# Seven block products in place of eight for two row pairs of the first gate and value chunks

## The chip, the cores and the metric

The program runs on one core of a Trainium2 chip. The metric is the device time of one execution in microseconds (us); lower is better.

## The reference, cut to what matters

A layer of a streaming encoder is computed for 256 tokens of width 2048. Its first step projects the normalised tokens by one wide weight matrix, and the first 4096 columns of that are the two halves of a gated unit:

```
h = rms_norm(x, norm_mix_g)                 # 256 x 2048
z = h @ w_in                                # 2048 x 9280 weights
u_conv, c_q, c_kv, k_pe, gate_logits = split(z)
a, gate = split(u_conv, 2)                  # 2048 columns each
h = a * sigmoid(gate)                       # then a depthwise convolution, and so on
```

Convolution, latent attention, a cross attention and a squared-ReLU MLP (width 8192) follow; the change leaves them alone.

## The kernel before

All engines are programmed by hand; every instruction's place on its queue is written out, and semaphores tie the queues together. The width 2048 is 16 tiles of 128 rows (`k`), the tokens are two halves of 128 (`t`), and the projection is made in chunks of 512 columns. Of chunk `i` the gate columns (`COL_G`) and the value columns (`COL_A`) are made one after the other, so 8 chunks of products make `u_conv`. A chunk's weights come in 8 **units** of two row tiles (128 x 1024, 512 KB). Unit `n` passes through these hands:

- SP loads it into slot `n % 4` of `raw` (`load`, L478). It first waits until VectorE is done with the unit four before.
- ScalarE (ACT) rounds it to the matmul's format, `whi` (`hi`, L717). It waits for the landing and until TensorE is done with the unit four before (`used`).
- VectorE (DVE) makes the rest, `wlo = raw - whi` (`lo`, L1213).
- TensorE (PE) multiplies (`unit`, L1979 to L1981): for each row tile and token half three matmuls, x high by w high, x high by w low, x low by w high, of 128 x 128 tokens by 128 x 512 weights; 12 matmuls a unit. Each token half has its own PSUM bank: 2 and 3 for the gate, 0 and 1 for the value.

The tokens arrive as rows (`x_in`, four chunks of 512 columns), and are transposed by TensorE (`turn`, L1992, 8 transposes a chunk into banks 6 and 7), scaled and rounded by ACT (`turn_out`, L734, `a_hi`) and split by DVE (`turn_low`, L1234, `a_lo`). `X_BEFORE` says before which units the chunks are turned, `X_AFTER` after which unit's `hi` and `lo` ACT and DVE take them out.

So the program's first stage is units 0 to 7 (gate, all 16 row tiles), a few small transposes into banks 5 and 4 (L2065, L2068), units 8 to 15 (value), and from unit 16 a loop over the other chunks that begins with a wait for `sg_ready`. Between the units ACT squares the tokens for the norm (`square_sums`, L749), takes the root (L758, with a table load) and, after unit 7, the sigmoid (L763); DVE multiplies at the end (`glu`, L1251). POOL loads small vectors and then computes the rotary angles (L631 to L654), which ACT needs at L825.

Later in the program, in the MLP, row pairs are already multiplied in Strassen's way, with seven products for eight. DVE makes the sums of four weight blocks in place (`t_sums`, L1830 to L1834), ACT rounds them (`t_high`, L1115), DVE splits them (`t_low`, L1839); sums of the tokens are made likewise, and the results are mixed out of PSUM (`m_sums`, L1846 to L1854). Their rows serve as prices here. "Rows" of the weights below means row tiles.

Of the kernel before, what the change touches and what calls it, by code (L numbers as in the profile page):

```python
# [8 lines left out]
ALU = mybir.AluOpType  # L9
# [8 lines left out]
P = 128  # L18
D = 2048
# [105 lines left out]
X_BEFORE, X_AFTER = (1, 3, 5), (2, 4, 6)  # L125
# [33 lines left out]
SLOTS = 3  # L159
B11, B12, B21, B22 = T1, T3, T4, T2 = range(4)  # L160
# [67 lines left out]
def build(nc, x, mem, positions, norm_mix_g, w_in, b_gate, conv_w, conv_b, conv_ln_g, conv_ln_b,  # L228
# [9 lines left out]
    with ExitStack() as ctx:  # L238
# [32 lines left out]
        sq_x = at(o + nbytes([P, D]), "sq_x", [P, TT, D])  # L271
# [63 lines left out]
        cy_copy = at(c_base + 28672, "cy_copy", [P, TT, NC])  # L335
        early = Sevens(cw_sum, ((cs_c[0], cs_m[0]), (cs_c[2], cs_m[2])), ((cs_c[1], cs_m[1]), (cs_c[3], cs_m[3])),
# [12 lines left out]
        rows = take("rows", [P, 2, TT, NC])  # L349
        qz = at(o, "qz", [P, 2, SEQ])  # L350
# [66 lines left out]
        ckv_whole = sem("ckv_whole")  # L417
        kpe_out, kpe_ready, kpe_prod, kpe_rotated, kpe_turned, kpeT_ready = (sem(n) for n in ("kpe_out", "kpe_ready", "kpe_prod", "kpe_rotated", "kpe_turned", "kpeT_ready"))
# [55 lines left out]
        def _(sp):  # L474
# [23 lines left out]
            for k in range(1, UPC):  # L498
                load(U_CONV + k, 0, w_in[:, 2 * k:2 * k + 2, COL_G:COL_G + NC])
                if k in (1, 2, 4):  # L500
                    load_x((1, 2, 4).index(k) + 1)
            load_chunk(U_CONV + UPC, 0, w_in, COL_A)
# [46 lines left out]
            def load_blocks(g, j):  # L549
# [3 lines left out]
                if j < SLOTS:  # L553
                    sp.wait_ge(chunk_out, g * CH + N_FF)
                else:
                    sp.wait_ge(m_done, g * FJ + (j - SLOTS + 1))
# [36 lines left out]
        def _(pool):  # L593
# [35 lines left out]
            pool.dma_start(cw_rows[CONV_K:CONV_K + 1, :], conv_b).then_inc(cw_landed, 16)  # L629
            pool.wait_ge(pos_landed, 16)  # L630
# [72 lines left out]
            pool.wait_ge(m_done, FJ_ALL)  # L703
# [7 lines left out]
        def _(act):  # L711
# [77 lines left out]
            for k in range(1, UPC):  # L789
                hi(U_CONV + k)  # L790
                if k in X_AFTER:
                    c = X_AFTER.index(k) + 1
                    turn_out(T_X + c, a_hi, CPB * c, V_MIX)
# [318 lines left out]
            def t_high(g, j):  # L1112

                act.wait_ge(t_made, g * (3 * FJ) + 3 * (j + 1))
                act.activation(t_hi[j % SLOTS][:], t_raw[j % SLOTS][:], ACT.Copy).then_inc(t_hi_ready, 1)  # L1115

# [91 lines left out]
        def _(dve):  # L1208
# [113 lines left out]
            for k in range(1, UPC):  # L1322
                lo(U_CONV + k)
                if k in X_AFTER:
                    c = X_AFTER.index(k) + 1
                    turn_low(T_X + c, a_lo, a_hi, CPB * c, V_MIX)
            lo(8)
            for k in range(6, 2 * UPC):
                lo(U_CONV + k + LEAD)
                if k == 8:  # L1330
                    reciprocal(rs_x, sd_x, R_X)
                if k == 10:
                    dve.wait_ge(vec_turned, 2)
                    dve.tensor_copy(vec[:, KT:], ps[:, 5, KT:V_N]).then_inc(vec_ready, 1)
                    dve.wait_ge(cw_turned, 1)
                    dve.tensor_copy(cw[:].rearrange("p k s -> p (k s)"), ps[:, 4, :]).then_inc(conv_step, 1)
            dve.wait_ge(used, U_CONV + 2 * UPC)
            dve.wait_ge(sg_ready, 1)
            dve.wait_ge(rs_ready, R_X)
            glu()  # L1340
# [485 lines left out]
            def t_sums(g, j):  # L1826

                t, done = t_raw[j % SLOTS], 3 * j
# [821 lines left out]
```

## Time and profile before

| what | value |
|---|---|
| median of three runs | 1595.53 us (1595.01 to 1596.44) |
| the profiled execution's own time | 1594.99 us |
| its span, first to last instruction | 1592.7 us |
| busy PE / DVE / ACT / POOL | 1581.0 / 1309.1 / 902.9 / 94.2 us |
| granted TensorE clock, mean | 0.998 |

The span is what the trace covers; 2.3 us of the execution's own time lie around it. A busy PE does not mean that it is at its peak, since a matmul's row runs on after the next one has begun.

### The profile page before, as it was taken

What the parts mean: (1) busy time and instruction counts of PE and PEld (TensorE: products, weight loads), DVE (VectorE), ACT (ScalarE), POOL (GpSimd) and SP (SyncE); (2) the same over time, 40 slices, a digit from 0 to 9 for tenths busy, and PEclk for the clock granted to TensorE, in tenths of its full rate; (3) what the DMA queues carried; (4) which work ended last, traced back from release to release, by engine and by line L of the source; (5) the groups of instructions that cost most, each with busy time, mean ns of one, the idle gap of its engine ahead of it and who ended that gap; (6) DMA issues with size and microseconds to landing.
All of it is one profiled execution on the core that took longest, in us unless ns stands there. A gap on an engine that the chain in (4) does not pass through costs nothing.

```text
span 1592.7 us, 22193 instructions
## 1 busy us (share of the span) xinstructions
PE 1581.0 (99%) x7909; PEld 1341.3 (84%) x7909; DVE 1309.1 (82%) x1757; ACT 902.9 (57%) x1138; POOL 94.2 (6%) x174
## 2 busy tenths in 40 slices
PE   9999999999999999999999999999999999999997
PEld 7888888888888888888888888888888888888886
DVE  5588999999998998787997786886779776978687
ACT  7444456555555556754566666455655565546655
POOL 6500010000000000000000000000000000000001
PEclk9999999999999999999999999999999999999999
DMA  7666655655655666657664676888678867887694
GB/s 259 200 189 186 192 160 177 175 181 172 185 174 174 209 201 185 197 177 243 216 197 146 184 228 185 281 261 289 180 259 266 271 212 221 281 272 225 205 295 147
DMA packets 169581, 336.68 MB, mean 211 GB/s; under 512 B 10377, under 2 KB 23297, under 8 KB 169089
## 3 DMA queue, kind: packets, MB, share of 16 engines
q1 hardware_dynamic: 164608, 324.84, 65.0%
q0 software_dynamic: 4864, 10.80, 3.1%
q8 instruction: 50, 0.82, 0.2%
q14 instruction: 27, 0.22, 0.0%
q10 hardware_dynamic: 32, 0.01, 0.0%
HBM read 326.16 MB, written 2.10 MB: 206 GB/s over the span
## 4 chain that ended last, share of the span: by engine, by line
PE 98%; DVE 0%; ACT 0%; issue 0%; ACTq 0%; POOL 0%; POOLq 0%; DVEq 0%
PE ps L2566 15%; PE ps L1979 12%; PE ps L1981 12%; PE ps L1980 12%; PE ps L2257 9%; PE ps L2259 9%; PE ps L2258 9%; PE ps L2568 7%; PE ps L1992 1%; PE ps L2168 1%; PE ps L2393 1%; PE ps L2163 1%; PE ps L2146 1%; PE ps L2148 1%; PE ps L2147 1%; PE ps L2202 1%
## 5 line engine op out<-in xcount | busy, mean ns | idle before, releaser
L717 ACT ACTIVATE w_both<-raw 128x1024 fp32r<-128x1024 f32 x522 | 550.6, 1059 | 488.1 <-PE ps L1981 176.4
L1213 DVE TENSOR_TENSOR w_both<-raw,w_both 128x1024 fp32r<-128x1024 f32 x522 | 634.8, 1223 | 192.5 <-ACT w_both L717 190.4
L2566 PE MATMUL ps<-a_both,w_both 128*128 128x512 f32 x1024 | 321.6, 395 | 0.0
L1979 PE MATMUL ps<-w_both,a_both 128*128 128x512 f32 (+1 forms) x636 | 251.3, 395 | 0.1
L1981 PE MATMUL ps<-w_both,a_both 128*128 128x512 f32 (+1 forms) x636 | 247.0, 388 | 0.0
L1980 PE MATMUL ps<-w_both,a_both 128*128 128x512 f32 (+1 forms) x636 | 247.0, 388 | 0.0
L2568 PEld LDWEIGHTS ps<-a_both,w_both 128*128 128x128 f32 x1024 | 192.4, 188 | 45.4
L1274 DVE SCALAR_TENSOR_TENSOR acc<-hconv,cwk,acc 128x256 f32<-128x256 f32 x464 | 201.3, 488 | 7.7 <-PE ps L2202 7.6
L2568 PE MATMUL ps<-a_both,w_both 128*128 128x256 f32 x1024 | 201.1, 278 | 0.0
L2257 PE MATMUL ps<-w_both,c_hi 128*128 128x512 f32 x402 | 156.8, 390 | 0.0
L2259 PE MATMUL ps<-w_both,c_lo 128*128 128x512 f32 x402 | 156.4, 389 | 0.0
L2566 PEld LDWEIGHTS ps<-a_both,w_both 128*128 128x128 f32 x1024 | 156.2, 189 | 0.3
L2258 PE MATMUL ps<-w_both,c_hi 128*128 128x512 f32 x402 | 156.4, 389 | 0.0
L1981 PEld LDWEIGHTS ps<-w_both,a_both 128*128 128x128 f32 x636 | 119.4, 188 | 24.5
L1979 PEld LDWEIGHTS ps<-w_both,a_both 128*128 128x128 f32 x636 | 119.5, 188 | 23.1 <-issue 0.3
L1980 PEld LDWEIGHTS ps<-w_both,a_both 128*128 128x128 f32 x636 | 119.6, 188 | 22.5
L2257 PEld LDWEIGHTS ps<-w_both,c_hi 128*128 128x128 f32 x402 | 75.5, 188 | 16.2 <-DVE w_both L1213 0.8
L2259 PEld LDWEIGHTS ps<-w_both,c_lo 128*128 128x128 f32 x402 | 75.5, 188 | 15.8
L2258 PEld LDWEIGHTS ps<-w_both,c_hi 128*128 128x128 f32 x402 | 75.5, 188 | 15.4
L1839 DVE TENSOR_TENSOR t_lo<-t_raw,t_hi 128x2048 fp32r<-128x2048 f32 x31 | 71.0, 2291 | 13.7 <-ACT t_hi L1115 13.6
L1115 ACT ACTIVATE t_hi<-t_raw 128x2048 fp32r<-128x2048 f32 x31 | 59.1, 1906 | 1.7 <-DVE t_raw L1834 1.5
L697 POOL DMA_DIRECT2D xres<-m_sum x7 | 8.4, 1197 | 819.2 <-DVE xres L1675 819.2
(441 smaller groups left out, 2243.3 us busy)
## 6 DMA issues: line engine op xcount, KB each, us to landing
raw<-in_w_ff_dram SPq DMA_DIRECT2D x225, 512.0 KB, 4.6
raw<-in_w_in_dram SPq DMA_DIRECT2D x137, 512.0 KB, 3.9
t_raw<-in_w_ff_dram SPq DMA_DIRECT2D x31, 1024.0 KB, 7.2
raw<-in_w_mla_out_dram SPq DMA_DIRECT2D x32, 512.0 KB, 4.3
raw<-in_w_conv_out_dram SPq DMA_DIRECT2D x32, 512.0 KB, 4.4
raw<-in_w_out_dram SPq DMA_DIRECT2D x32, 512.0 KB, 4.5
raw<-in_w_ukv_dram SPq DMA_DIRECT2D x16, 512.0 KB, 3.8
raw<-in_w_xkv_dram SPq DMA_DIRECT2D x16, 512.0 KB, 4.0
```

The costliest lines, as they stand in the source:

```text
L717: act.activation(whi[:, s, :], raw[:, s, :], ACT.Copy).then_inc(hi_ready, 1)
L1213: dve.tensor_tensor(wlo[:, s, :], raw[:, s, :], whi[:, s, :].bitcast(F32), ALU.subtract).then_inc(lo_ready, 1)
L1274: ins = dve.scalar_tensor_tensor(out=to, in0=h[:, tap:tap + SEQ], scalar=cwk[:, tap:tap + 1], in1=to, op0=ALU.mult, op1=ALU.add)
L1839: dve.tensor_tensor(t_lo[j % SLOTS][:], t_raw[j % SLOTS][:], t_hi[j % SLOTS][:].bitcast(F32), ALU.subtract).then_inc(t_lo_ready, 1)
L1979: pe.matmul(sum_, x_hi[:, k0 + k, tok], w_hi, start=(first and k == 0), stop=False)
L1980: pe.matmul(sum_, x_hi[:, k0 + k, tok], w_lo, start=False, stop=False)
L1981: mm = pe.matmul(sum_, x_lo[:, k0 + k, tok], w_hi, start=False, stop=(last and k == kts - 1))
L2257: pe.matmul(ps[:, bank, :], x_hi, w_hi, start=first, stop=False, skip_group_check=True)
L2258: pe.matmul(ps[:, bank, :], x_hi, w_lo, start=False, stop=False, skip_group_check=True)
L2259: return pe.matmul(ps[:, bank, :], x_lo, w_hi, start=False, stop=last, skip_group_check=True)
L2566: pe.matmul(both, whi[:, s, cols[n]], a_both[:, :, k0 + k, :], start=(first and k == 0), stop=False)
L2568: mm = pe.matmul(ps[:, b0 + b + n, 0:SEQ], wlo[:, s, cols[n]], a_hi[:, k0 + k, :], start=False, stop=(last and k == 1))
```

## The change

Gate and value chunks of the first 512 columns are computed together. Rows 0 to 11 go as before (gate units 0 to 5, value units 6, 7, 8, 11, 14, 15). For the two row pairs 12/13 and 14/15 the four blocks (gate and value columns of an even and an odd row) are multiplied by both token halves in seven block products (21 matmuls) where eight (24) stood. A pair takes two slots, `left` (units 9 and 12, the two gate blocks, 6 matmuls) and `right` (units 10 and 13, the odd value block, 3 matmuls from the slot and 12 from the weight sums).

For this, SP loads the pair's four blocks once more, raw, into `e_raw` (two loads of 512 KB behind unit 5 and two behind unit 8); DVE makes three sums of them (`e_sums`), ACT rounds (`e_high`, 128 x 2048), DVE splits (`e_low`). ACT takes the last token chunk out of PSUM twice, rounded and whole (`turn_out_whole`), behind unit 7 instead of 6; DVE makes the tokens' sums (`eh_sums`), ACT rounds, DVE splits. The squares and the root move from behind units 7 and 8 to behind unit 14. The gate is no longer ready after unit 7: it is mixed from five banks by `em_sums` behind unit 16's `lo`, the sigmoid runs on the mixed rows, the small transposes wait for the mixing (they use its banks), and POOL's angles wait for the last product of the pairs.

```
-X_BEFORE, X_AFTER = (1, 3, 5), (2, 4, 6)
+X_BEFORE, X_AFTER = (1, 3, 5), (2, 4, 7)
+EM = 2
+E_PLAIN = KT - 2 * EM
+E_UNITS = ([("gate", m) for m in range(E_PLAIN // 2)]
+           + [("value", 0), ("value", 1), ("value", 2), ("left", 0), ("right", 0), ("value", 3), ("left", 1), ("right", 1), ("value", 4), ("value", 5)])
+E_LOAD = {5: 0, 8: 1}
+E_M1, E_M7, E_M6, E_M5 = 4, 5, 6, 7
...
+                if n in E_LOAD:
+                    j = E_LOAD[n]
...
+                    kts = slice(E_PLAIN + 2 * j, E_PLAIN + 2 * j + 2)
+                    sp.dma_start(e_raw[j % SLOTS][:, B11:B21 + 1:2, :], w_in[:, kts, COL_G:COL_G + NC]).then_inc(t_landed[j % SLOTS], 16)
+                    sp.dma_start(e_raw[j % SLOTS][:, B12:B22 + 1:2, :], w_in[:, kts, COL_A:COL_A + NC]).then_inc(t_landed[j % SLOTS], 16)
...
+            pool.wait_ge(m_done, EM)
             pool.wait_ge(pos_landed, 16)
...
-            square_sums(sq_x, x_in, ss_x)
-            hi(8)
-            act.wait_ge(ss_ready, SS_X)
-            root(sd_x, ss_x, D)
-            for k in range(6, 2 * UPC):
-                hi(U_CONV + k + LEAD)
-                if k == 9:
-                    act.wait_ge(used, U_CONV + UPC)
-                    act.wait_ge(rs_ready, R_X)
-                    glu_gate()
...
+            for n in range(1, 2 * UPC + LEAD):
+                if n < 2 * UPC and E_UNITS[n][0] == "right":
+                    hi_second(U_CONV + n, 0)
+                else:
+                    hi(U_CONV + n)
...
+                if n == 8:
+                    e_high(0)
+                if n == 9:
+                    eh_high(0)
+                if n == 12:
+                    e_high(1)
+                if n == 14:
+                    for t in range(TT):
+                        wait(act, ss_ready, t)
+                        act.activation(sq_x[:], x_in[:, t, :], ACT.Square, accum_out=ss_x[:, t:t + 1]).then_inc(ss_ready, 1)
+                    act.wait_ge(ss_ready, SS_X)
+                    root(sd_x, ss_x, D)
+                if n == 16:
+                    act.wait_ge(used, U_CONV + 2 * UPC - 3)
+                    act.activation(rows[:, 1, 0, :], ps[:, E_M1, :], ACT.Copy).then_inc(em_copied, 1)
+            act.wait_ge(sg_ready, 1)
...
+            def em_sums():
+
+                both, minus = rows[:, 1, :, :], rows[:, 0, :, :]
+                dve.wait_ge(em_copied, 1)
+                dve.wait_ge(m_done, EM)
+                dve.tensor_tensor(both[:, 1, :], ps[:, E_M6, :], both[:, 0, :], ALU.add).then_inc(em_made, 1)
...
+                dve.tensor_tensor(both, ps[:, 2:4, :], both, ALU.add).then_inc(sg_ready, 1)
+
+            for n in range(1, 2 * UPC + LEAD):
+                if n == 2 * UPC + 1:
+                    em_sums()
...
+                if n == 7:
+                    e_sums(0)
+                if n in X_AFTER:
+                    c = X_AFTER.index(n) + 1
                     turn_low(T_X + c, a_lo, a_hi, CPB * c, V_MIX)
...
+                if n == 8:
+                    eh_sums(0)
+                if n == 9:
+                    eh_low(0)
+                    e_low(0)
+                if n == 11:
+                    e_sums(1)
+                if n == 16:
                     reciprocal(rs_x, sd_x, R_X)
...
+                if n == 13:
+                    e_low(1)
...
+                elif kind == "right":
+                    pe.wait_ge(eh_lo_ready, m // 2 + 1)
+                    product(0, *e_combined(3, m), *e_slot(n, 1)).then_inc(used, 1)
...
+                    pe.wait_ge(t_lo_ready, m + 1)
+                    product(E_M6, *e_combined(1, m), *e_weight(T2, m), first=(m == 0), last=(m == EM - 1))
...
+            pe.wait_ge(em_made, 4)
             pe.wait_ge(vec_landed, 16 * 7)
```

**DVE between the last token chunk and the sums of the second pair.** Before, the low halves of the chunk (L1234), five units' `lo` in a row, and the reciprocal of the norm:

```order
L1234 SCALAR_TENSOR_TENSOR a_both<-ps,vec,a_both 128x256 [waits turn_hi]
L1234 SCALAR_TENSOR_TENSOR a_both<-ps,vec,a_both 128x256
L1213 TENSOR_TENSOR w_both<-raw,w_both 128x1024 [waits hi_ready] x5
L1241 RECIPROCAL stat<-stat 128x2 [waits sd_ready]
L1213 TENSOR_TENSOR w_both<-raw,w_both 128x1024 [waits hi_ready] x2
```

Now, from unit 8's `lo` on (L1282); the weight sums of the first pair and the chunk's low halves stand just ahead of these rows, behind unit 7's `lo`:

```order
L1282 TENSOR_TENSOR w_both<-raw,w_both 128x1024 [waits hi_ready]
L1397 TENSOR_TENSOR eh_sum_153<-e_act 128x256 [waits turn_hi]
L1398 TENSOR_TENSOR eh_sum_153<-e_act 128x256
L1400 SCALAR_TENSOR_TENSOR eh_sum_153<-eh_sum_153,e_act 128x256 [waits eh_made]
L1402 TENSOR_TENSOR eh_sum_153<-e_act,eh_sum_153 128x256 [waits eh_made]
L1282 TENSOR_TENSOR w_both<-raw,w_both 128x1024 [waits hi_ready]
L1407 TENSOR_TENSOR eh_lo_155<-eh_sum_153,eh_hi_151 128x1024 [waits eh_hi_ready]
L1422 TENSOR_TENSOR e_lo_145<-e_raw_142,e_hi_148 128x2048 [waits t_hi_ready]
L1288 TENSOR_TENSOR w_both<-raw,w_both 128x512 [waits hi_ready]
L1282 TENSOR_TENSOR w_both<-raw,w_both 128x1024 [waits hi_ready]
L1413 TENSOR_TENSOR e_raw_143<-e_raw_143 128x1024 [waits t_landed1]
```

Six instructions now stand between unit 8's `lo` and the half `lo` of unit 10 (L1288) that the first pair's `right` products wait for, besides unit 9's own.

**ACT around the squares.** Before, behind unit 7's `hi`:

```order
L717 ACTIVATE w_both<-raw 128x1024 [waits used,landed3]
L749 ACTIVATE sq_x,stat<-x_in 128x2048 x2
L717 ACTIVATE w_both<-raw 128x1024 [waits used,landed0]
L758 ACT_TABLE_LOAD
L758 ACTIVATE stat<-stat 128x2 [waits ss_ready]
L717 ACTIVATE w_both<-raw 128x1024 [waits used,landed1]
```

Now, from the rounding of the second pair's weight sums (L840) to the copy of the first mixed bank (L867); the L750 in the middle are units 14, 15 and 16:

```order
L840 ACTIVATE e_hi_149<-e_raw_143 128x2048 [waits t_made]
L757 ACTIVATE w_both<-raw 128x512 [waits used,landed1]
L750 ACTIVATE w_both<-raw 128x1024 [waits used,landed2]
L862 ACTIVATE sq_x,stat<-x_in 128x2048
L862 ACTIVATE sq_x,stat<-x_in 128x2048 [waits ss_ready]
L791 ACT_TABLE_LOAD
L791 ACTIVATE stat<-stat 128x2 [waits ss_ready]
L750 ACTIVATE w_both<-raw 128x1024 [waits used,landed3]
L750 ACTIVATE w_both<-raw 128x1024 [waits used,landed0]
L867 ACTIVATE rows<-ps 128x512 [waits used]
```

Both squares, the table load and the root stand between units 14 and 15, with no unit in between.

**PE at the small transposes.** Before, between the gate's last unit and the value's first:

```order
L1981 MATMUL ps<-w_both,a_both 128x512
L2065 MATMUL ps<-ident,vec_rows 128x104 [waits vec_ready,vec_landed]
L2068 MATMUL ps<-ident,cw_rows 128x32 [waits cw_landed]
L2068 MATMUL ps<-ident,cw_rows 128x32 x15
L1979 MATMUL ps<-w_both,a_both 128x512 [waits lo_ready]
```

Now, between unit 15 and the loop over the other chunks:

```order
L2193 MATMUL ps<-w_both,a_both 128x512
L2247 MATMUL ps<-ident,vec_rows 128x104 [waits vec_ready,vec_landed,em_made]
L2250 MATMUL ps<-ident,cw_rows 128x32 [waits cw_landed]
L2250 MATMUL ps<-ident,cw_rows 128x32 x15
L2254 UNCONDITIONAL_BRANCH
L2108 ISA [waits sg_ready]
L2114 MATMUL ps<-w_both,a_both 128x512 [waits lo_ready]
```

The transposes have gained a wait for `em_made`, the fourth of DVE's mixing sums; all later work of PE is queued behind it.

## Rows read from the trace of the kernel before

**Rows 1.** The page: span, and each engine's busy time.

```profile
span 1592.7 us, 22193 instructions
PE 1581.0 (99%) x7909; PEld 1341.3 (84%) x7909; DVE 1309.1 (82%) x1757; ACT 902.9 (57%) x1138; POOL 94.2 (6%) x174
```

**Rows 2.** Waits of PE's weight loads from 11 us on: total us, times, longest.

```profile
PEld ps L2257 <- DVE w_both L1213: 0.8, 2, 0.4
...
```

**Rows 3.** Timeline of PE: start us, us, engine, line, operation, shapes.

```profile
32.39 0.25 PE L2065 MATMUL ps<-ident,vec_rows 104*128 104x104 f32 x1
...
33.68 0.50 PE L1979 MATMUL ps<-w_both,a_both 128*128 128x512 f32 x1
...
36.53 0.39 PE L1979 MATMUL ps<-w_both,a_both 128*128 128x512 f32 x1
...
54.90 0.39 PE L1979 MATMUL ps<-w_both,a_both 128*128 128x512 f32 x1
```

**Rows 4.** Stretch of the start: PE, PEld, DVE, ACT, POOL busy, PEclk, DMA share, GB/s.

```profile
11.00:19.00 8.00, 7.87 (x40) 6.30 (x38) 5.81 (x10) 5.98 (x11) 1.98 (x4) 1.00 1.06 388
```

**Rows 5.** Issue of units 7 and 8 on SP's timeline, KB and us to landing.

```profile
16.00 0.37 SPq L478 DMA_DIRECT2D raw<-in_w_in_dram  x1
raw<-in_w_in_dram SPq DMA_DIRECT2D x1, 512.0 KB, 4.4
17.36 0.37 SPq L478 DMA_DIRECT2D raw<-in_w_in_dram  x1
raw<-in_w_in_dram SPq DMA_DIRECT2D x1, 512.0 KB, 5.8
```

**Rows 6.** DMA queues from 17 to 24 us: packets, MB, share of 16 engines.

```profile
...
q8 instruction: 1, 0.02, 1.0%
```

**Rows 7.** Timeline of ACT: copying out a chunk, a square, the root, two `hi`.

```profile
23.97 1.57 ACT L734 ACTIVATE a_both<-ps,vec 128x256 fp32r<-128x256 f32 x4 [2.90 <-PE ps L1992]
...
26.36 1.93 ACT L749 ACTIVATE sq_x<-x_in 128x2048 f32<-128x2048 f32 x1
...
31.23 1.28 ACT L758 ACT_TABLE_LOAD   x1
32.52 0.30 ACT L758 ACTIVATE stat<-stat 128x2 f32<-128x2 f32 x1
32.73 2.00 ACT L717 ACTIVATE w_both<-raw 128x1024 fp32r<-128x1024 f32 x2
```

**Rows 8.** Timeline of DVE in the first stage: two `lo`, a chunk, a wait.

```profile
20.16 2.36 DVE L1213 TENSOR_TENSOR w_both<-raw,w_both 128x1024 fp32r<-128x1024 f32 x2
24.84 1.66 DVE L1234 SCALAR_TENSOR_TENSOR a_both<-ps,vec,a_both 128x256 fp32r<-128x256 f32 x4 [2.32 <-ACT a_both L734]
...
31.25 1.23 DVE L1213 TENSOR_TENSOR w_both<-raw,w_both 128x1024 fp32r<-128x1024 f32 x1 [3.50 <-ACT w_both L717]
```

**Rows 9.** DVE in the MLP: three weight sums, then `lo`; four mixing sums, then the next.

```profile
916.87 1.22 DVE L1830 TENSOR_TENSOR t_raw<-t_raw 128x1024 f32<-128x1024 f32 x1
...
919.46 2.36 DVE L1213 TENSOR_TENSOR w_both<-raw,w_both 128x1024 fp32r<-128x1024 f32 x2
...
1024.47 0.68 DVE L1846 TENSOR_TENSOR m_sum<-ps,m_sum 128x512 f32<-128x512 f32 x1
...
1027.11 1.22 DVE L1675 TENSOR_TENSOR xres<-ps,xres 128x1024 f32<-128x1024 f32 x1
```

**Rows 10.** By tile: rounding and splitting of weight sums, token sums (ns min/median/max).

```profile
L1115 ACT ACTIVATE t_hi<-t_raw x31: 1897/1902/1925, 920.0 to 1555.7; 128x2048 fp32r<-128x2048 f32 x31
L1839 DVE TENSOR_TENSOR t_lo<-t_raw,t_hi x31: 2284/2292/2296, 921.9 to 1557.8; 128x2048 fp32r<-128x2048 f32 x31
L1531 DVE TENSOR_TENSOR h_sum<-h_sum,ps x2: 420/421/422, 716.2 to 717.0; 128x256 f32<-128x256 f32 x2
```

**Rows 11.** POOL's angles by tile, and ACT's use of them on its timeline.

```profile
L645 POOL TENSOR_SCALAR rope_tmp<-rope_tmp x12: 372/374/1371, 26.6 to 61.2; 128x64 f32<-128x64 f32 x12
203.25 0.31 ACT L825 ACTIVATE rope_cs<-rope_cs 128x128 f32<-128x128 f32 x1
```

More of the change, by code:

```diff
@@ L159 @@
 SLOTS = 3
+E_BLOCKS = [len(range(n, EM, SLOTS)) for n in range(SLOTS)]
 B11, B12, B21, B22 = T1, T3, T4, T2 = range(4)
@@ L804, in _ @@
+            act.wait_ge(sg_ready, 1)
+            act.wait_ge(rs_ready, R_X)
+            for t in range(TT):
+                last = act.activation(rows[:, 1, t, :], rows[:, 1, t, :], ACT.Sigmoid, scale=rs_x[:, t:t + 1])
+            last.then_inc(em_copied, 1)
             act.wait_ge(consts, 4)
@@ L1337, in _ @@
             dve.wait_ge(used, U_CONV + 2 * UPC)
-            dve.wait_ge(sg_ready, 1)
+            dve.wait_ge(em_made, 4)
+            dve.tensor_tensor(rows[:, 0, :, :], ps[:, 0:2, :], rows[:, 0, :, :], ALU.add).then_inc(em_made, 1)
+            dve.wait_ge(em_made, 5)
+            dve.wait_ge(em_copied, 2)
             dve.wait_ge(rs_ready, R_X)
-            glu()
+            for t in range(TT):
+                last = dve.scalar_tensor_tensor(out=rows[:, 0, t, :], in0=rows[:, 0, t, :], scalar=rs_x[:, t:t + 1],
+                                                in1=rows[:, 1, t, :], op0=ALU.mult, op1=ALU.mult)
@@ L2054, in _, with product @@
             first_product(1, 1, a_lo, whi).then_inc(used, 1)
-            for k in range(1, UPC):
-                if k in X_BEFORE:
-                    c = X_BEFORE.index(k) + 1
+            def product(bank, x_hi, x_lo, w_hi, w_lo, first=False, last=False):
+                pe.matmul(ps[:, bank, :], x_hi, w_hi, start=first, stop=False, skip_group_check=True)
+                pe.matmul(ps[:, bank, :], x_hi, w_lo, start=False, stop=False, skip_group_check=True)
+                return pe.matmul(ps[:, bank, :], x_lo, w_hi, start=False, stop=last, skip_group_check=True)
@@ L2058, in _ @@
+            for n in range(1, 2 * UPC):
+                if n in X_BEFORE:
+                    c = X_BEFORE.index(n) + 1
                     pe.wait_ge(x_landed[c], 16)
                     turn(T_X + c, x_in, NC * c, split_out(T_X + c - 1))
-                pe.wait_ge(turn_lo, k + 1)
-                unit(U_CONV + k, 0, a_hi, a_lo, 2 * k, 2, k == 0, k == UPC - 1)
+                kind, m = E_UNITS[n]
+                left, right = E_PLAIN + 2 * m, E_PLAIN + 2 * m + 1
+                if kind == "gate":
+                    pe.wait_ge(turn_lo, n + 1)
+                pe.wait_ge(lo_ready, U_CONV + n + 1)
+                if kind == "gate":
+                    for k in range(2):
+                        for t in range(TT):
+                            mm = product(2 + t, *tokens(2 * m + k, t), *e_slot(n, k))
+                    mm.then_inc(used, 1)
+                elif kind == "left":
+                    pe.wait_ge(turn_lo, left // 2 + 1)
+                    product(E_M1, *tokens(left, 0), *e_slot(n, 0), first=(m == 0), last=(m == EM - 1))
+                    product(2, *tokens(right, 0), *e_slot(n, 1), last=(m == EM - 1)).then_inc(used, 1)
+                elif kind == "right":
+                    pe.wait_ge(eh_lo_ready, m // 2 + 1)
+                    product(0, *e_combined(3, m), *e_slot(n, 1)).then_inc(used, 1)
+                    if m == 0:
+                        pe.wait_ge(turn_lo, 2 * CH)
+                    pe.wait_ge(t_lo_ready, m + 1)
+                    product(E_M6, *e_combined(1, m), *e_weight(T2, m), first=(m == 0), last=(m == EM - 1))
+                    product(3, *tokens(right, 1), *e_weight(T4, m), last=(m == EM - 1))
+                    product(E_M5, *e_combined(0, m), *e_weight(T1, m), first=(m == 0), last=(m == EM - 1))
+                    product(E_M7, *e_combined(2, m), *e_weight(T3, m), first=(m == 0), last=(m == EM - 1)).then_inc(m_done, 1)
+                else:
+                    for k in range(2):
+                        for t in range(TT):
+                            mm = product(t, *tokens(2 * m + k, t), *e_slot(n, k), first=(m == 0 and k == 0), last=(n == 2 * UPC - 1 and k == 1))
+                    mm.then_inc(used, 1)
@@ L2070, in _ @@
             tr.then_inc(cw_turned, 1)
-            for k in range(UPC):
-                unit(U_CONV + UPC + k, 0, a_hi, a_lo, 2 * k, 0, k == 0, k == UPC - 1)
             with pe.Fori(1, CH) as i:
```

142 lines of the change are left out of this document (105 added, 37 removed).

## The prediction

> **What bounds the kernel now.** I read the page first: PE is busy for 1581.0 us of a span of 1592.7, DVE for 1309.1 [rows 1]. Busy is not the same as full, so the second look is at PE's waits. From 11 us on the longest kind adds up to 0.8 us in two places [rows 2], so PE is fed all the way and every matmul that goes is worth its step in the stream. The step is read from starts, not from durations: from 36.53 to 54.90 us stand 81 steps [rows 3], 0.2268 us each, while one row lasts 0.39. The third look is at who feeds PE in the first stage. DMA runs at 388 GB/s, full, up to 19 us [rows 4]; ACT and DVE had room, with DVE idle 3.50 us before one `lo` [rows 8]. The change spends that room. So the question is whether DVE and ACT, in the new order, still keep ahead of PE.
>
> **The gain.** Seven products for eight, for two pairs: 2 x 3 = 6 matmuls less, 6 x 0.2268 = 1.36 us. Nothing else leaves PE: the chunk turns stay at units 1, 3 and 5 and the small transposes (32.39 to 33.68, 1.29 us [rows 3]) only move. 1.36 us is the most that can be won, and 0.2% of the time, about what a measurement of this kernel can tell from no change, is 3.2 us.
>
> **When PE would get there.** Before, unit 9 starts at 36.53, behind nine units and the transposes, so unit 16 starts at 36.53 + 84 x 0.2268 = 55.58. Now, with no wait, the first `right` would start at 36.53 - 1.29 + 6 x 0.2268 = 36.60, the transposes at 55.58 - 1.29 - 1.36 = 52.93, unit 16 at 54.22.
>
> **What SP adds.** Unit 7 was issued at 16.00 and landed 4.4 us later, at 20.4 [rows 5]. The first `e_raw` block, two loads of 512 KB, now goes ahead of units 6 and 7 into a queue that is full: 2 x 524 KB / 388 GB/s = 2.7 us [rows 4], so unit 7 lands at 23.1. That is the lower bound. The upper one comes from unit 8, which took 5.8 instead of 4.4 us [rows 5] though it moves no more: in that stretch an instruction load [rows 6] and POOL's small vectors come in between, and a unit has landed only when all sixteen parts have. If the same 1.4 to 1.5 us hit the longer queue, unit 7 lands at 24.6. I take 24.0, nearer to the row with the disturbance, since the queue now has work behind it throughout that stretch and the lost time can't be made up in an idle moment as before.
>
> The Trainium skill ("DMA: Bandwidth & Descriptors", Issuing engines are not separate DMA queues) says that transfers run on the same 16 engines and interleave, whichever engine started them. It speaks against the change: POOL's loads would take their turns out of the new block's time. The late unit 8 agrees. By the queue's bytes alone the sum below is +2.0 us; with the disturbance it is +2.9.
>
> **What DVE and ACT add: one chain from that landing to the transposes.** Steps are start to start. `hi` of unit 7 takes 1.06, so its `lo` starts 1.1 after the landing. DVE then never waits: `lo` 7 1.14 (2.36 for two, of which the last lasts 1.22 [rows 8]); the weight sums 2.59 (916.87 to 919.46 [rows 9]); the chunk's low halves 1.6 [rows 8]; `lo` 8 1.14; the tokens' sums four times 0.42 [rows 10], overlapped 1.5; `lo` 9 1.14; `eh_low`, of `lo`'s shape, 1.14; `e_low` 2.2 (2.29 [rows 10] less the overlap); half of a `lo` for unit 10, 0.6. Sum 13.1, and the half `lo` ends 14.2 after the landing. Had unit 7 landed at 23.1 that is 37.3: the first `right` waits 0.8; with 24.0 it waits 1.7.
>
> On: `lo` 11 1.14 and the second weight sums 2.59 end 18.0 after the landing. Now ACT is the one that is waited for: it rounds the sums (1.90 [rows 10], step 1.8), unit 13's half 0.55, unit 14's `hi` 0.95 (2.00 for two [rows 7]), two squares of 1.93 and a handoff 3.95, table load and root 1.28 + 0.30 [rows 7], stepping in 1.5, `hi` of unit 15 1.06: 9.8, at 27.8. Then DVE: `lo` 15 and 16 2.3, the reciprocal 0.15, four mixing sums (1024.47 to 1027.11 [rows 9]) with the last one's end 2.75: at 33.0, with handoffs 33.1. The copy of the first bank on ACT hides beside `lo` 16, the double copy of the last chunk (four pieces 1.57 [rows 7], so eight 3.1) beside the weight sums; without that cover it would cost the 1.6.
>
> Nothing in this chain waits for PE, so its length stands: the transposes can start at 24.0 + 33.1 = 57.1, unit 16 at 58.4 to 58.5, against 55.58: **+2.9 us**. With 23.1 it is +2.0, with 24.6 +3.5. Seen from PE these are four waits: about 1.7 at the first `right`, 1.0 at the second pair's sums (its `e_low` ends some 2.3 behind the sums' rounding), 0.3 at unit 15, whose `lo` stands behind the squares, and 1.2 at the transposes; 4.2 less 1.36. Each earlier wait only shortens the later ones; the last one sets the end.
>
> After that PE is not late again: `lo` 17 ends 2.3 behind the fourth mixing sum (the fifth, of 1.22, and its own 1.14), and is wanted 1.3 + 2.7 behind it; sigmoid, product and copies stand ahead of `lo` 19, wanted some 10 us behind it. So the shift stays as it is to the end. POOL's new wait moves the angles by some 27 us, from 23 to 50; ACT wants them at 203.25, and twelve of their operations lie from 26.6 to 61.2 [rows 11], so they end by some 95 and 100 us are spare.
>
> The bounds of the rest: some thirty steps, each read to about 0.03 us, make 0.9 us either way if all err to one side. With the landing's bounds the chain gives +1.1 to +4.4. The profiled execution took 1594.99 us, 2.3 around its span; with 2.9 it would be 1597.9, and the median lies 0.54 above that execution: **1598.4 us**.
>
> **Rivals.**
>
> *DVE and ACT keep up, and the saving shows.* Then no wait is left and the time is 1595.5 - 1.4 = 1594.2. It decides at one point: the fourth mixing sum must end by 52.9, so the chain would have to be 29.8 us long instead of 33.1 even with the earliest landing. For it speaks that the kernel's own rows of the same steps in the MLP run hidden; against it that there they stand among units with slack, and that the sum has no idle time left to squeeze. 1 in 9.
>
> *The landing is later, or the steps longer than read.* Unit 7 at 24.4 or later, or the added work on DVE slowed, makes it +3.2 or more, over 0.2%: 1599.3 or so (+3.8). For it speaks unit 8's row; against it that the disturbance lasted some 3 us there and may fall behind unit 7. 3 in 10.
>
> *POOL against DVE.* POOL's angles used to run beside a DVE with room; now they run from 50 us on, into the convolution's sums. One POOL operation goes from 372 ns to 1371 [rows 11] while a DVE subtraction is under way, so the two hold each other up; if DVE lost 0.1 us on each of four instructions of a unit, `lo` would fall behind 0.4 us a unit less its idle time, and over some fifteen units PE could wait 1 to 2 us more, 1600. The Trainium skill ("GPSIMD Engine Reference", Specifications) says that POOL shares its SBUF interface with VectorE and contends with instructions that have two SBUF inputs, as these have. It is POOL that the row shows late, not DVE. 1 in 50.
>
> **Chances and range.** The forecast, +1.1 to +3.2: 0.57; later and over +3.2: 0.30; the saving shows: 0.11; POOL: 0.02. The forecast and the saving both lie within 0.2%, which makes 0.67 same and 0.31 slower; nothing worked out here reaches -3.2, and I leave 0.02 for it. For eight in ten the range goes from just under the forecast's low end, where part of the saving would show, to +4.6: 1595.6 to 1600.1.
>
> **What would show it.** Right: in the changed profile PE has gaps of a microsecond or two ahead of the first `right`'s product and ahead of the transposes, the latter ended by a mixing sum; DVE has no idle time from unit 7's `lo` to the second weight sums; unit 7 lands near 24; unit 16 starts near 58.5; from there the two traces run parallel. Wrong: PE fed through, with unit 16 at 54.2; a wait of DVE for a landing in the middle of the chain; gaps on PE after 60 us. The prediction fails if the chain's steps overlap better than read one by one, or if DVE's work on the new tiles costs other than on the MLP's.

## The result, and the profile after

| | before | after |
|---|---|---|
| median of 13 runs each | 1595.44 us (1595.01 to 1596.44) | 1599.52 us (1598.82 to 1601.51) |
| the profiled execution's own time | 1594.99 us | 1599.33 us |
| its span | 1592.7 us | 1597.5 us |
| granted TensorE clock, mean | 0.998 | 0.997 |

The ratio is 1.0026, with a 95% interval of 1.0017 to 1.0034: 4.1 us slower, where 2.9 was forecast.

The same view as [rows 2], PE's weight loads of the changed kernel and what they waited for from 11 us on (total us, times, longest):

```profile
PEld ps L2191 <- DVE w_both L1288: 2.7, 1, 2.7
PEld ps L2191 <- DVE w_both L1282: 1.6, 4, 0.6
PEld ps L2247 <- DVE rows L1435: 1.0, 1, 1.0
```

Two waits are new, and both are where the prediction put one: L1288 is the half `lo` of the first `right`, L1435 the fourth mixing sum, for which the transposes wait. The waits expected at the second pair's sums and at unit 15 are missing; a small one ahead of unit 8, 0.3 us of PE's time, was not forecast. PE's timeline, which answers to [rows 3], shows the two, and one thing that nobody expected:

```profile
36.47 0.39 PE L2193 MATMUL ps<-w_both,a_both 128*128 128x512 f32 x1
39.10 0.79 PE L2191 MATMUL ps<-w_both,eh_hi 128*128 128x512 f32 x1 [2.25 <-DVE w_both L1288]
39.70 0.63 PE L2192 MATMUL ps<-w_both,eh_hi 128*128 128x512 f32 x1
40.12 0.63 PE L2193 MATMUL ps<-w_both,eh_lo 128*128 128x512 f32 x1
...
42.26 0.49 PE L2192 MATMUL ps<-e_lo,a_both 128*128 128x512 f32 x1
42.59 0.40 PE L2193 MATMUL ps<-e_hi,a_both 128*128 128x512 f32 x1
42.82 0.40 PE L2191 MATMUL ps<-e_hi,eh_hi 128*128 128x512 f32 x1
...
56.91 0.39 PE L2193 MATMUL ps<-w_both,a_both 128*128 128x512 f32 x1
57.85 0.31 PE L2247 MATMUL ps<-ident,vec_rows 104*128 104x104 f32 x1 [0.56 <-DVE rows L1435]
...
59.20 0.50 PE L2114 MATMUL ps<-w_both,a_both 128*128 128x512 f32 x1
```

The first `right` starts 2.63 us behind its predecessor, so it waited 2.4. Then eight steps take 3.49 us (39.10 to 42.59) instead of 1.81: most are 0.43 us. Stretches of the start give the reason (columns as in [rows 4]; the clock is the first number behind POOL's):

```profile
36.00:39.00 3.00, 0.85 (x4) 0.38 (x2) 3.00 (x4) 1.40 (x2) 0.00 (x0) 1.00 0.33 87
39.00:42.40 3.40, 3.30 (x8) 2.62 (x9) 3.33 (x5) 0.00 (x0) 0.00 (x0) 0.51 0.62 180
42.40:46.00 3.60, 3.60 (x17) 2.96 (x16) 2.23 (x4) 3.19 (x3) 0.00 (x0) 0.99 0.54 155
```

After the wait PE was granted half its clock, 1.2 GHz in place of 2.4, for 3.4 us. Of the 1.7 us more, 0.1 is the slower second step behind any wait (0.34 for 0.23 us elsewhere), the rest the clock's. Unit 16 starts at 59.20, against 55.58 before: +3.6.

The feeders, on ACT's and DVE's timelines (answers to [rows 7, 8]):

```profile
24.82 1.06 ACT L750 ACTIVATE w_both<-raw 128x1024 fp32r<-128x1024 f32 x1 [2.05 <-DMA raw<-in_w_in_dram]
...
42.80 1.92 ACT L840 ACTIVATE e_hi<-e_raw 128x2048 fp32r<-128x2048 f32 x1 [5.40 <-DVE e_raw L1417]
...
51.64 2.00 ACT L750 ACTIVATE w_both<-raw 128x1024 fp32r<-128x1024 f32 x2
```

```profile
25.91 1.23 DVE L1282 TENSOR_TENSOR w_both<-raw,w_both 128x1024 fp32r<-128x1024 f32 x1 [1.89 <-ACT w_both L750]
27.05 1.22 DVE L1413 TENSOR_TENSOR e_raw<-e_raw 128x1024 f32<-128x1024 f32 x1
...
38.36 0.69 DVE L1288 TENSOR_TENSOR w_both<-raw,w_both 128x512 fp32r<-128x512 f32 x1
...
42.08 0.69 DVE L1417 TENSOR_TENSOR e_raw<-e_raw 128x512 f32<-128x512 f32 x1
...
45.27 0.69 DVE L1288 TENSOR_TENSOR w_both<-raw,w_both 128x512 fp32r<-128x512 f32 x1 [1.37 <-ACT w_both L757]
...
52.72 2.38 DVE L1282 TENSOR_TENSOR w_both<-raw,w_both 128x1024 fp32r<-128x1024 f32 x2 [3.41 <-ACT w_both L750]
...
57.12 0.68 DVE L1435 TENSOR_TENSOR rows<-rows,ps 128x512 f32<-128x512 f32 x1
```

Unit 7's `hi` had been waiting for its landing, which came at 24.80, and starts at 24.82. From 25.91 to 42.08 DVE shows no wait. The fourth mixing sum ends at 57.12 + 0.68 = 57.80. So the chain from landing to fourth sum is 33.0 us long; 33.1 was forecast.

Why was the landing 24.80 and not 24.0? In the traces a transfer's semaphore rises in sixteen steps, as many as the core has DMA engines. Of unit 7's steps fifteen had come by 23.42, the last at 24.80. The queues from 17 to 24 us, as in [rows 6]:

```profile
q0 software_dynamic: 174, 0.04, 3.2%
q8 instruction: 1, 0.02, 1.0%
```

Queue 8's one packet, 16 KB of instructions, began at 21.15 and took 1.1 us on one engine. Before, it began at 19.66, and unit 8's steps show the same: fifteen by 22.06, the last at 23.19. There nobody waited for unit 8.

The lateness is carried on while the queue has work. In the changed kernel the last step of units 8, 9, 10 and 11 still comes 1.0 to 1.2 us behind the fifteenth, and only that of unit 12, issued at 32.46 as the queue runs out, 0.1. Before, with a gap in the queue ahead of it, unit 9 is already free of it.

### The profile page after: what moved, and what is told of

It is laid out like the page before. It is cut to its first block, busy times and chain, and to the rows that moved or that the text cites. A ratio compares the mean times of both kernels' runs of the same rounds, so it can differ in the third digit from the quotient of the medians.

```text
span 1597.5 us, 22220 instructions
## 1 busy us (share of the span) xinstructions
PE 1582.3 (99%) x7903; PEld 1340.9 (84%) x7903; DVE 1325.0 (83%) x1776; ACT 908.7 (57%) x1146; POOL 97.8 (6%) x174
## 4 chain that ended last, share of the span: by engine, by line
PE 93%; DVE 3%; ACT 1%; DMA 1%; issue 1%; SPq 0%; ACTq 0%; DVEq 0%
PE ps L2740 15%; PE ps L2114 11%; PE ps L2116 11%; PE ps L2115 11%; PE ps L2191 9%; PE ps L2193 9%; PE ps L2192 9%; PE ps L2742 7%; PE ps L2127 1%; DMA raw<-in_w_in_dram 1%; DVE w_both L1282 1%; PE ps L2347 1%; PE ps L2567 1%; PE ps L2342 1%; PE ps L2325 1%
## 5 line engine op out<-in xcount | busy, mean ns | idle before, releaser
L750 ACT ACTIVATE w_both<-raw 128x1024 fp32r<-128x1024 f32 x520 | 548.6, 1059 | 479.0 <-PE ps L2116 165.6
L1282 DVE TENSOR_TENSOR w_both<-raw,w_both 128x1024 fp32r<-128x1024 f32 x520 | 631.8, 1222 | 182.6 <-ACT w_both L750 180.3
L2114 PE MATMUL ps<-w_both,a_both 128*128 128x512 f32 (+1 forms) x576 | 227.7, 395 | 0.0
L2116 PE MATMUL ps<-w_both,a_both 128*128 128x512 f32 (+1 forms) x576 | 223.7, 388 | 0.0
L2115 PE MATMUL ps<-w_both,a_both 128*128 128x512 f32 (+1 forms) x576 | 223.6, 388 | 0.0
L2116 PEld LDWEIGHTS ps<-w_both,a_both 128*128 128x128 f32 x576 | 108.1, 188 | 22.2
L2115 PEld LDWEIGHTS ps<-w_both,a_both 128*128 128x128 f32 x576 | 108.3, 188 | 20.3
L2114 PEld LDWEIGHTS ps<-w_both,a_both 128*128 128x128 f32 x576 | 108.2, 188 | 20.3
```

The costliest lines, as they stand in the source:

```text
L750: act.activation(whi[:, s, :], raw[:, s, :], ACT.Copy).then_inc(hi_ready, 1)
L1282: dve.tensor_tensor(wlo[:, s, :], raw[:, s, :], whi[:, s, :].bitcast(F32), ALU.subtract).then_inc(lo_ready, 1)
L2114: pe.matmul(sum_, x_hi[:, k0 + k, tok], w_hi, start=(first and k == 0), stop=False)
L2115: pe.matmul(sum_, x_hi[:, k0 + k, tok], w_lo, start=False, stop=False)
L2116: mm = pe.matmul(sum_, x_lo[:, k0 + k, tok], w_hi, start=False, stop=(last and k == kts - 1))
```

## The experiments

The theory: everything hangs on one chain of DVE and ACT work that begins with unit 7's landing and ends with the fourth mixing sum; PE's own losses before that are absorbed. The rivals: PE's losses set the end (the halved clock above all); or the loads alone do, whatever is done with them. All medians are of 5 to 11 runs, each group beside 21 to 33 runs of the kernel before (1595.59, 1595.54 and 1595.46 us).

| experiment | median us | less before | ratio, 95% interval |
|---|---|---|---|
| block's loads behind unit 7 | 1599.98 | +4.4 | 1.0030 (1.0018 to 1.0042) |
| squares behind unit 18 | 1598.21 | +2.6 | 1.0017 (1.0008 to 1.0026) |
| PE kept busy ahead of the first `right` | 1601.12 | +5.5 | 1.0035 (1.0022 to 1.0049) |
| loads and squares | 1596.98 | +1.4 | 1.0010 (1.0001 to 1.0019) |
| the same, second block behind unit 10 | 1596.09 | +0.55 | 1.0004 (0.9995 to 1.0013) |
| the same, other order on DVE and ACT | 1596.21 | +0.67 | 1.0005 (0.9996 to 1.0014) |
| squares, PE kept busy | 1598.49 | +2.95 | 1.0019 (1.0010 to 1.0028) |
| before, with two unused loads | 1595.75 | +0.21 | 1.0001 (0.9992 to 1.0010) |
| changed, POOL's loads late | 1599.23 | +3.8 | 1.0026 (1.0017 to 1.0035) |
| second pair rounded later | 1594.73 | -0.73 | 0.9996 (0.9987 to 1.0005) |

**The block's loads behind unit 7.**

```
-E_LOAD = {5: 0, 8: 1}
+E_LOAD = {7: 0, 8: 1}
```

> The first e_raw block is loaded behind unit 7 instead of behind unit 5; nothing else differs from the changed kernel. Chain theory (the shift is the landing of unit 7 plus 33.0 us of DVE and ACT work): unit 7 lands near 20.4 as in the kernel before, the block near 24.5, so that the weight sums start near 24.5 instead of 27.05 and the fourth mixing sum ends near 55.3 instead of 57.8: 2.3 to 2.6 us faster than the changed kernel, 1597.0 us. If the added bytes as such cost the time, whatever waits for them, there is no change, 1599.5.

1599.98, nothing gained. Unit 7 did land at 20.75, as said. DVE's timeline shows where the chain was caught again:

```profile
24.66 1.22 DVE L1413 TENSOR_TENSOR e_raw<-e_raw 128x1024 f32<-128x1024 f32 x1 [0.61 <-DMA e_raw<-in_w_in_dram]
...
33.07 1.23 DVE L1282 TENSOR_TENSOR w_both<-raw,w_both 128x1024 fp32r<-128x1024 f32 x1 [1.58 <-ACT w_both L750]
```

The weight sums start 2.4 earlier, but now `lo` of unit 9 waits: unit 9 lands at 31.96, behind four block loads in a row. Of the 2.4 us, 0.7 arrive at the fourth mixing sum (57.09). The timetable behind the 1597.0 had unit 9 earlier; that step was wrong. The profiled execution, which kept the full clock at the first `right`, took 1598.51; see the clock below for the others.

**The squares late.** Squares, root and reciprocal go behind unit 18.

```
-                if n == 14:
+                if n == 18:
                     for t in range(TT):
...
-                if n == 16:
+                if n == 2 * UPC + 2:
                     reciprocal(rs_x, sd_x, R_X)
```

> Squares, root and the reciprocal stand behind unit 18 instead of 14 and 16; nothing else differs from the changed kernel. Chain theory: 5.4 us of ACT work leave the chain, the mixing sums are done before PE wants the transposes, and the shift is then what PE itself lost at the first right unit: its 2.4 us wait and some 1.9 us of slow matmuls less the 1.4 us saved. PE would reach the transposes at 56.9 instead of 57.85: 1.0 us faster than the changed kernel, 1598.5 us. If the slow stretch costs nothing once the chain is short, 2.5 to 3 us faster, 1596.8. If the squares were not on the chain, no change, 1599.5.

1598.21. This takes some 4 us of squares and 1.5 of the root out of the chain, and the fourth mixing sum ends at 54.69 (57.80 in the changed kernel). Of PE's waits only the first is left:

```profile
PEld ps L2191 <- DVE w_both L1288: 2.4, 1, 2.4
```

The fourth sum is 3.1 earlier, the time 1.3, because in this trace PE's own losses now set the end: the wait and the halved clock behind it. In the changed kernel the chain hid them, so it was the chain that set the end there.

**PE kept busy ahead of the first `right`.** Eight products by the identity into a free bank, before the wait.

```
+                if kind == "right" and m == 0:
+                    for _ in range(8):
+                        pe.matmul(ps[:, E_M7, 0:P], ident[:], ident[:], start=True, stop=True)
                 pe.wait_ge(lo_ready, U_CONV + n + 1)
```

> Eight small matmuls of the identity into a bank that is free are put ahead of PE's wait at the first right unit, so that PE works through most of that wait; they add no wait. Chain theory: TensorE keeps the full clock, PE comes to the transposes 1.6 to 1.9 us earlier and waits that much longer for the mixing sum; the time stays at 1599.5 within 0.3. If the slow clock at the first right unit sets the end, 1.6 to 1.9 us faster, 1597.8.

1601.12, worse than both said; the profiled execution, with 1602.70, is the slowest of the five. At the first `right` the clock stayed; it fell behind the transposes' wait instead, as stretches of this kernel show:

```profile
56.00:59.90 3.90, 2.98 (x25) 2.24 (x24) 3.83 (x6) 2.11 (x3) 3.17 (x10) 1.00 0.78 253
59.90:63.40 3.50, 3.50 (x9) 2.74 (x9) 3.46 (x4) 1.83 (x3) 3.16 (x5) 0.51 0.45 118
```

There nothing comes behind it that could hide it. Nine steps from 59.67 on take 1.6 us more than they would at full clock, and unit 7 landed 0.35 later than in the changed kernel; together that is most of the 2.1 us by which PE's stream is behind that of the changed kernel at 70 us. The mean granted clocks of the single executions point the same way. One stretch such as this takes 3.4 x 0.5 us from a mean over 1597, 0.001. With this edit, the one execution at 0.998 took 1599.77 and the four at 0.996 and 0.997 took 1601.11 to 1602.70. With the loads behind unit 7, two at 0.998 took 1598.51 and 1599.42, four at 0.997 took 1599.76 to 1601.22. The changed kernel itself doesn't care: five at 0.998 have a median of 1599.66, eight lower ones 1599.26. The sorting is rough, though. Every profile also ends with a stretch at 1.2 GHz, of 4.9 to 8.3 us, whose length moves the mean by up to 0.001 as well; and of the kernel with POOL's loads late (below), which has the same chain, five at 0.998 have a median of 1599.09 and six lower ones lie from 1598.37 to 1601.25. The fastest of those six is the profiled one, with the stretch at the first `right`. So it is an estimate that the halved clock costs some 1.5 us in the first two kernels, and nothing where the chain ends later anyway.

**Loads and squares together.** The first two edits.

> Both edits at once: the first block behind unit 7, and squares, root and reciprocal behind unit 18. Chain theory: the first right unit waits 0.4 us or less, the clock stays full, the transposes wait for nothing; what is left is about 1 us at the second pair's weight sums, against 1.36 saved: between the kernel before and 0.5 us over it, 1595.2 to 1596.0 us. If PE loses its time to something else than these waits (more loads, other banks), more than 1597.

1596.98, where 1596.0 at most was expected. Unit 9's landing holds here too, at 31.65:

```profile
32.77 1.23 DVE L1282 TENSOR_TENSOR w_both<-raw,w_both 128x1024 fp32r<-128x1024 f32 x1 [1.38 <-ACT w_both L750]
```

PE's weight loads wait 1.3 at the first `right` and 1.1 at the second pair's sums; PE itself loses 1.2 and 0.9 there. Less the saving of 1.36 that is +0.8; unit 16 starts at 56.70, +1.1, in an execution whose first full `lo` was 0.25 late, and +1.4 was measured. This execution is the slowest of the eleven (1599.06): PE ends 1.8 us behind before, and DVE, by a delay in the last 50 us that this edit doesn't reach, 3.7.

**The second block's loads behind unit 10.** In addition to those two edits:

```
-E_LOAD = {7: 0, 8: 1}
+E_LOAD = {7: 0, 10: 1}
```

> The changed kernel with the late squares, the first block's loads behind unit 7 and the second block's loads moved from behind unit 8 to behind unit 10. If unit 9's landing (31.65 us, behind four block loads) now holds the chain, unit 9 lands near 29, VectorE's 1.4 us wait before unit 9's rounding error goes, TensorE's 1.3 us wait before the first right product goes with it, the fourth mixing sum ends near 51.7, and the time is 1595.7 us (1595.3 to 1596.3). If VectorE's own order of work holds the first right product, the wait stays and the time is that of the kernel with both edits, 1597.0. The wait at the second pair's weight sums (1.05 us) stays in both.

1596.09: unit 9 lands at 29.17, DVE's wait is gone, and with it PE's at the first `right`. Only one is left on PE's timeline, a step of 1.00 us from 44.95:

```profile
45.95 0.50 PE L2191 MATMUL ps<-e_hi,eh_hi 128*128 128x512 f32 x1 [0.62 <-DVE e_lo L1422]
```

**Another order on DVE and ACT.** The second block behind unit 9; `hi` and `lo` of unit 10 right behind those of unit 9, and the second weight sums ahead of unit 11's `lo`.

> As the kernel before this one, with the second block behind unit 9, unit 10's rounding and rounding error ahead of the first pair's operand and weight errors, and the second block's weight sums one unit earlier on VectorE. If what is left of the loss is the order in which VectorE and ScalarE prepare the first two pairs, both waits at the right products together fall to 0 to 0.6 us and the time is 1594.8 us (1594.2 to 1595.3), the saving of 1.36 us less what is left of a wait. If the four block loads (2.7 us of the queue) cost more than the timetable has, the waits move to units 9 to 12 and the time stays above 1595.5.

1596.21. The wait at the second pair went, and others came: PE's steps are 0.60 at the first pair's weight errors and 1.03 at unit 11's `lo`, the longest of the next row. What was started earlier on DVE made the work behind it late, and the whole 1.36 is given back.

```profile
PEld ps L2199 <- DVE w_both L1286: 2.2, 3, 1.1
```

**Squares late and PE kept busy.**

> The changed kernel with the late squares and with eight identity products on TensorE ahead of the first right product's wait. If the stretch of half clock behind that wait (39.45 to 42.86 us with late squares) costs its slow matmuls now that no later wait hides them, it goes and takes about 1.6 us with it: 1596.6 us (1596.2 to 1597.2). If the matmuls of that stretch are held by something else, or the stretch only moves to another wait, the time stays that of the late squares, 1598.2.

1598.49: no gain, where 1596.6 was expected. The profile has no such stretch, all executions stand at 0.998, and in the profile the transposes come 0.95 earlier than with late squares alone. It is 0.95 and not 1.6 since at full clock PE reaches the second pair earlier, where its weight load waits 1.1 and PE loses 0.9, which the slow matmuls had covered. Of the 0.95, 0.7 are lost again, 0.6 of them between 660 and 820 us, where this execution's weight loads wait twice as long as the 0.8 of [rows 2]:

```profile
PEld ps L2191 <- DVE w_both L1282: 1.5, 2, 0.8
```

In that place, which no edit reaches, the profiles of the other ten kernels lose between 0.0 and 0.4 us against that of before. Why this one loses more is open. So the trace shows the slow steps, but that they cost time with the late squares is not shown by the times.

**Before, with two unused loads.** The kernel before with 2 x 512 KB behind unit 5, which nothing reads (DVE waits for them once, some 20 us after they landed).

```
+                if k == 5:
+                    for c in range(2):
+                        sp.dma_start(x_raw[:, 2 * c:2 * c + 2, :], w_in[:, 12:14, ...]).then_inc(extra_landed, 16)
```

> The kernel before with two more loads of 512 KB each behind unit 5, that nothing uses: the changed kernel's transfers without its work. If the block's loads alone push unit 7, it lands at 24.6 to 24.9 us in place of 20.36, by the bytes alone at 23.1; TensorE wants unit 7 only near 31 us and unit 8 near 34, so the time stays 1595.5 us (1595.0 to 1596.0). If later units' landings are pushed far enough that TensorE waits for them, it is up to 2.7 us more, 1598.2.

1595.75: the loads alone cost nothing that can be told. Unit 7 landed at 25.30, and here too one step was late: fifteen by 23.66. By 33 us ACT stands 0.54 behind [rows 7] (32.73), but the first DMA landings of this execution were late already, and DVE's first full `lo` starts at 10.57, where the profile of before has it at 9.90.

```profile
33.27 1.99 ACT L722 ACTIVATE w_both<-raw 128x1024 fp32r<-128x1024 f32 x2
```

```profile
10.57 1.23 DVE L1218 TENSOR_TENSOR w_both<-raw,w_both 128x1024 fp32r<-128x1024 f32 x1
```

So single profiles differ by up to 0.7 us before any of this work, and differences between them are read only behind that.

**POOL's loads late.** The changed kernel with

```
             pool.wait_ge(x_landed[CH - 1], 16)
+            pool.wait_ge(lo_ready, U_CONV + 10)
```

> The changed kernel, with GpSimd's ten small loads (0.3 MB between 17 and 27 us) held back until unit 9's rounding error is done near 34 us. In the changed kernel fifteen of unit 7's sixteen shares land by 23.42 us and the last at 24.80; by the bytes all would land at 23.07. If the 1.1 us load of instructions on one DMA engine makes the last share late and GpSimd's loads only the 0.35 us of the fifteen, unit 7 lands at 24.2 to 24.5 us, the chain is 0.3 to 0.6 us earlier, and the time is 1599.1 us (1598.8 to 1599.4). If GpSimd's packets also make the last share late, it lands at 23.1 to 23.6, the fourth mixing sum ends near 56.4, and the time is 1598.0 (1597.7 to 1598.5). A time of 1599.5 with a landing before 24.4 would speak against the chain from unit 7's landing.

1599.23, and unit 7 landed at 24.17. The last row of the chain is

```profile
56.47 0.68 DVE L1436 TENSOR_TENSOR rows<-rows,ps 128x512 f32<-128x512 f32 x1
```

which ends at 57.15: 32.98 behind the landing, as in the changed kernel (33.00). The landing itself says less than was expected of it, since executions start unequally. Counted from unit 5's landing it came 6.74 us later; the five profiles that have POOL's loads and the same queue show 7.17 (changed), 6.62 (squares late), 7.17 (PE kept busy), 6.27 (both) and 7.38 (before with unused loads). Four transfers of 524 KB at 388 GB/s make 5.4. So 0.9 to 2.0 us are added with POOL's loads and 1.3 without them: in the last step a share of POOL's loads can't be told from the scatter, and the instruction load, 1.1 us on one engine in all of them, is the cause that is left. In the fifteenth step such a share can be told: it came 5.40 us behind unit 5's landing here, just what the bytes make, and 5.65 to 5.79 in the five. So POOL's loads add some 0.25 to 0.4 us to the other parts, by one execution without them.

**The second pair rounded later.** On top of the kernel with the second block behind unit 10:

```
-                if n == 12:
+                if n == 13:
                     e_high(1)
```

> The kernel with late squares, the first block behind unit 7 and the second behind unit 10, with the second pair's rounding moved one unit later on ScalarE, behind unit 13's. If the 1.0 us wait at the second pair's weight sums comes from VectorE standing 1.36 us before unit 13's rounding error, whose rounding waits on ScalarE behind the second pair's, that wait goes and nothing replaces it: 1595.1 us (1594.7 to 1595.6), the first time below that of the kernel before (1595.54). If the second pair's errors are then late because its rounding starts later, a wait of 0.5 to 1.0 us stays there and the time is 1595.6 to 1596.1.

1594.73. ACT now rounds unit 13's half while it would have waited for the sums, DVE's 1.36 us before that `lo` go, and PE runs through to unit 16:

```profile
52.98 0.39 PE L2193 MATMUL ps<-w_both,a_both 128*128 128x512 f32 x1
53.21 0.25 PE L2247 MATMUL ps<-ident,vec_rows 104*128 104x104 f32 x1
...
54.50 0.50 PE L2114 MATMUL ps<-w_both,a_both 128*128 128x512 f32 x1
```

Unit 16 starts at 54.50, 1.08 ahead of before; and this execution's first full `lo` was 0.26 late, so up to there 1.34 is saved:

```profile
10.16 1.23 DVE L1282 TENSOR_TENSOR w_both<-raw,w_both 128x1024 fp32r<-128x1024 f32 x1
```

Not all of it lasts. The first matmul of the next chunk stands 0.82 ahead, in this kernel and before:

```profile
63.71 0.50 PE L2114 MATMUL ps<-w_both,a_both 128*128 128x512 f32 x1
...
64.53 0.48 PE L1979 MATMUL ps<-w_both,a_both 128*128 128x512 f32 x1
```

The last matmul of the program stands 0.70 ahead. 0.1 us is the slower second step behind the transposes, which before stood at unit 8 (33.68, [rows 3]). Another 0.2 or so is lost between 60 and 100 us in each of the six profiles with late squares, and in none of the others of the changed kernel: the late squares are not quite free.

All its 11 times lie from 1594.50 to 1595.32, those of before from 1594.97 to 1596.43. The interval of the ratio still takes in no change.

## Why the prediction was right, step by step

**The gain: right, as the most that can be won.** 1.36 us was forecast for six matmuls; the last kernel shows 1.34 up to unit 16, and about 1.0 to the end (0.70, and the 0.26 of its late start).

**The landing: the term that was mis-sized.** 24.0 was taken between 23.1 and 24.6; it was 24.80, just beyond the upper bound. The disturbance was there, one step of sixteen that came 1.4 us behind the others; the error was to take less than its full size because it might fall elsewhere. That lost time isn't made up in a queue that has work throughout, the prediction's reason, is what units 8 to 11 show. Of its two causes in the prediction the instruction load is the one that shows in the single late step. The Trainium skill ("DMA: Bandwidth & Descriptors", Issuing engines are not separate DMA queues) says that transfers of all issuers interleave on the same engines, which made POOL's loads a suspect; the one run without them puts their price at 0.25 to 0.4 us in the other parts, and in the last one it can't be told.

**The chain: right, link by link.** Behind the landing, the first half `lo` ends at 14.25 (forecast 14.2), the second weight sums at 17.97 (18.0), unit 15's `hi` at about 27.9 (27.8), the fourth mixing sum at 33.00 (33.1). The rows of the MLP's sums [rows 9, 10] held as prices. With the measured landing in it, the forecast's own sum gives +3.7, and unit 16 stands at +3.6.

**The waits: the sum right, the split wrong.** 1.7, 1.0, 0.3 and 1.2 were forecast, 4.2 in all, or 5.0 with the measured landing. Measured are 0.3 ahead of unit 8, where none was forecast, 2.4 at the first `right`, then 1.7 of slow matmuls, nothing at the second pair and at unit 15, and 0.7 at the transposes: 5.1. The one at the first `right` is larger by the landing's 0.8; the slow matmuls delayed PE by what it would otherwise have waited for. The fall of the clock has no place in the prediction. That the sum still holds is due to the chain, which sets the end as long as PE is there before it, and PE was there by 0.7 us.

**The rivals.** That the saving shows failed by 4.9 us: the fourth sum ended at 57.8, not 52.9. That the landing is later, with 3 in 10, is what came: it said 24.4 or more and about +3.8, and 24.80 and +4.1 were measured. So the forecast's own stretch, +1.1 to +3.2, was missed, and only the range takes the result in. POOL against DVE showed on DVE and not on PE. Over all 464 of the convolution's multiply-adds the mean hides it (489 ns, before 488). The first 27 of them run beside POOL's angles now, and did not before; here they are in the changed kernel and in the kernel before (count, busy us, mean ns, idle us):

```profile
L1343 DVE SCALAR_TENSOR_TENSOR acc<-hconv,cwk,acc 128x256 f32<-128x256 f32 x27 | 12.8, 525 | 0.0
...
L1274 DVE SCALAR_TENSOR_TENSOR acc<-hconv,cwk,acc 128x256 f32<-128x256 f32 x27 | 11.4, 478 | 0.0
```

DVE loses 47 ns on each of them, 1.3 us in all, about half of what the rival supposed for one instruction; it has the room, and PE's shift against before is the same at 70 and at 200 us. The angles end at 99.20 and are used at 207.00.

**What stays open.** From the first chunk to the end the two profiles drift apart by another 0.5 us, most of it in two places, near 788 and 1051 us. The kernel with the unused loads shows 0.4 of the same near 785, and the kernel with POOL's loads late, which has all the block products, only 0.1 to the end. So, as far as these profiles show, it goes with the single profile and not with the block products; what makes it was not tried. Open too is what the halved clock costs in the time, and why the gain of the squares with PE kept busy doesn't show there.

## What to carry to other kernels

Find the first thing that a moved load makes late, and follow everything behind it on the same engines: here a 1.4 us saving on PE was spent by a chain of DVE and ACT work that begins with one unit's landing, and 2 x 512 KB ahead of that unit in a full queue made it begin late. Then look for work in the chain that is wanted late (the squares), loads that can go behind what is wanted sooner, and one rounding that stands in front of another engine's next operation; such moves, none of which touches the arithmetic, turned +4.1 into -0.7, though the interval of the last still takes in no change. Shortening one link shows only as far as the next cause allows, so the edits had to be read together. And a mean over all instructions of a kind can hide what happens to the few that have met a new neighbour.

## What was not expected of the hardware

After a wait of 1.9 to 2.4 us at the first `right`, PE was granted 1.2 GHz for 3.4 us in each of the three profiles that have such a wait (the changed kernel, late squares, POOL's loads late); waits of 1.1 and 1.4 us there, in the two kernels with the block behind unit 7 and the second behind unit 8, left it at 2.4 GHz. Behind a wait of 1.1 us at the transposes it fell in one profile (PE kept busy) and not in another (block behind unit 7), so the length of one wait doesn't decide alone; what else does was not tried. Each stretch makes PE's steps 1.6 us longer in all. What that costs in the end depends on what is late behind it: nothing in the changed kernel, some 1.5 us, by the estimate above, with PE kept busy.

A load of 16 KB of the program's own instructions, 1.1 us on one of sixteen DMA engines, made the last of sixteen parts of a 512 KB transfer come 0.6 to 1.6 us behind the fifteen others; which unit is hit first depends on when the load falls (unit 8 before, unit 7 after, unit 6 in the run with PE kept busy), and the units behind it stay late as long as the queue has work (8 to 11 after).

POOL and DVE held each other up: a POOL operation of 372 ns took up to 1371 [rows 11], and 27 DVE multiply-adds of 478 ns took 525 on the mean, up to 628, beside POOL's angles.
